# Four PSUM slots for attention scores in tiles 0 to 3, and four score units in a row behind a group's last transposition

## The reference, cut to what matters

```python
s_c = einsum('btghd,bngd->bghtn', qg, kc) * scale + bias       # compressed blocks of 64 keys
s_s = einsum('btghd,bgtkcd->bghtkc', qg, k_s) * scale + bias   # selected blocks (16 of 16 here: all earlier keys)
s_w = einsum('btghd,bkgd->bghtk', qg, kw) * scale + bias       # a window of 512 keys
p = softmax(where(allowed, s, -1e30)); o = p @ v               # for each of the three
y = (g_c * o_c + g_s * o_s + g_w * o_w) * silu(z)
```

## Time and profile before

| what | value |
|---|---|
| median of three executions | 1130.91 us (1128.89 to 1138.05) |
| the profiled execution | 1135.59 us, span 1133.8 us, mean granted TensorE clock 0.958 |
| PE busy | 1067.4 us, 94% of the span |
| DVE, ACT, POOL busy | 585.9, 450.5, 180.7 us |
| prompt attention | from 353.2 us (first score) to about 648 us |

### The profile page before, as it was taken

The page is one execution under the profiler, slowest core; times in us unless marked ns, Lnnn a source line. Parts: engine busy times, 40 slices in busy tenths (PEclk is TensorE's granted clock), DMA queues, the critical chain, the costliest instruction groups (busy, mean ns, idle before and its releaser), DMA issues. The chain is left out here.

```text
span 1133.8 us, 15415 instructions
## 1 busy us (share of the span) xinstructions
PE 1067.4 (94%) x5985; PEld 931.0 (82%) x5985; DVE 585.9 (52%) x1121; ACT 450.5 (40%) x761; POOL 180.7 (16%) x259
## 2 busy tenths in 40 slices
PE   6999999999998889999999888999999999999996
PEld 4889889999997667787777675788799899998884
DVE  4544221123322468787788534544589756555213
ACT  4331121110033457677667504122257655564101
POOL 2110568000004222220200000000112000000000
PEclk9999999999998689999999955999999999999999
DMA  8361002121114000000002620322320111131222
GB/s 295 118 211 63 19 4 63 38 55 39 39 38 149 1 1 1 1 1 1 1 12 64 203 96 1 130 79 94 108 65 19 38 56 39 38 149 61 84 89 79
DMA packets 64566, 74.82 MB, mean 66 GB/s; under 512 B 13793, under 2 KB 48657, under 8 KB 64494
## 3 DMA queue, kind: packets, MB, share of 16 engines
q1 hardware_dynamic: 61902, 70.77, 19.6%
q0 software_dynamic: 2496, 3.04, 0.8%
q10 hardware_dynamic: 96, 0.03, 0.0%
HBM read 62.19 MB, written 16.34 MB: 69 GB/s over the span
## 5 line engine op out<-in xcount | busy, mean ns | idle before, releaser
L1380 PE MATMUL ps<-h1T_hi,w_c_hl 128*128 128x352 f32 x768 | 148.7, 326 | 2.6 <-DVE h1T_lo L2265 1.5
L1380 PE MATMUL ps<-hT_hi,w_fm_hl 128*128 128x352 f32 x768 | 145.5, 324 | 1.5 <-DVE region_w L1988 1.5
L1380 PEld LDWEIGHTS ps<-h1T_hi,w_c_hl 128*128 128x128 f32 x768 | 127.9, 188 | 4.8 <-ACT region_w L1347 1.7
L1384 PE MATMUL ps<-ident,region_w 128*128 128x128 f32 (+2 forms) x730 | 117.7, 290 | 14.6 <-ACT region_w L1194 6.8
L1380 PEld LDWEIGHTS ps<-hT_hi,w_fm_hl 128*128 128x128 f32 x768 | 127.4, 188 | 2.0 <-issue 2.0
L1384 PEld LDWEIGHTS ps<-ident,region_w 128*128 128x128 f32 (+2 forms) x730 | 95.6, 151 | 39.8 <-DVE p_hl L2166 9.3
L2166 DVE TENSOR_TENSOR p_hl<-ps,p_hl 128x512 fp32r<-128x512 f32 x132 | 91.2, 691 | 60.4 <-ACT p_hl L1202 58.9
L1202 ACT CAST p_hl<-ps 128x512 fp32r<-128x512 f32 x132 | 77.1, 584 | 78.8 <-PE ps L1384 78.3
L1380 PE MATMUL ps<-p_hl,v_hl 128*128 128x512 f32 x264 | 96.9, 449 | 7.1 <-DVE p_hl L2166 2.8
L1194 ACT ACTIVATE region_w<-region_w,negm 128x640 f32<-128x640 f32 (+7 forms) x128 | 94.0, 736 | 8.6 <-DVE negm L2141 7.2
L2141 DVE CUSTOM_DVE_ANT_0 region_w<-ps,region_w 128x640 f32<-128x640 f32 (+7 forms) x128 | 88.6, 699 | 5.8 <-PE ps L1380 5.4
(11 more groups left out here) (309 smaller groups left out, 1803.0 us busy)
## 6 DMA issues: line engine op xcount, KB each, us to landing
region_w<-in_x_prompt SPq DMA_DIRECT2D x16, 512.0 KB, 3.7
region_w<-in_w_in_c SPq DMA_DIRECT2D x16, 512.0 KB, 3.8
region_w<-in_w_in_a SPq DMA_DIRECT2D x12, 512.0 KB, 3.8
rel_rows_dram<-rel_line_dram SPq DMA_DIRECT2D x8, 576.0 KB, 12.8
region_y<-in_w_in_a SPq DMA_DIRECT2D x8, 512.0 KB, 6.4
region_w<-rel_rows_dram SPq DMA_DIRECT2D x16, 256.0 KB, 5.1
region_w<-in_w_out_a SPq DMA_DIRECT2D x2, 2048.0 KB, 12.4
x_dram<-region_w SPq DMA_DIRECT2D x8, 512.0 KB, 2.6
```

What stands on the lines that cost most here:

```text
L1380: return nc.tensor.matmul(out, l, r, start=start, stop=stop, skip_group_check=True)
L1384: return nc.tensor.transpose(out, x, ident[0:k, 0:k])
```

## The change

The score units of tiles 0 to 3 (units 0 to 67, none over 512 keys) get four slots of one bank each; unit n waits for the reading of unit n-4. From unit 68 on the two slots of two banks stay; unit 68 waits for unit 64, and unit 69 for unit 67. `FEW` goes from 2 to 4, and with it the order in tiles 2 and 3: all units of group j+2 stand behind the last transposition of group j where group j+1 is of tiles 0 to 3.

```diff
-FEW = 2
+FEW = 4
+NARROW = 17 * (WIN // P)
+
+def score_slot(n):
+    return n % 4 if n < NARROW else 2 * (n % 2)
+
+def slot_free(n):
+    if n < NARROW + 1:
+        return max(0, n - 3)
+    return n - 1
...
-                    slot = 2 * (n % 2)
-                    if n >= 2:
-                        pe.wait_ge(logits_ready, n - 1)
+                    slot = score_slot(n)
+                    if slot_free(n):
+                        pe.wait_ge(logits_ready, slot_free(n))
...
-                    slot = 2 * (n % 2)
+                    slot = score_slot(n)
                     if n == HPG + 2:
                         v_low(1, v_w)
                     dve.wait_ge(scores_done, n + 1)
```

## The result

The changed kernel takes 1152.01 us (median of four runs, 1146.18 to 1153.41) where the kernel before, timed beside it, takes 1130.03: a ratio of 1.0181, 95% interval 1.0142 to 1.0221. It is slower, and above the range of the prediction. The profiled execution took 1150.86 us with a span of 1149.1.

A forecast was written before the change was run, and what follows sets the result against it. PE, busy 94% of the span, was taken as the bound. From the profiled 1135.6 us, -13.2 (slots), +12.2 (bunch) and +1.6 (clock) gave 1136.2, less 4.7 for the median: 1131.5 us, range 1124 to 1139.

The forecast's parts named there:

- Tiles 0 and 1, four slots: Tiles 0 and 1: units start earlier, with fewer waits for readings and less time at the low clock; 13.2 us gained.
- the new wait ahead of the fifth unit: Tile 2's first bunch has five units; the fifth, S38, waits for the reading of S34: 2.1 us.
- Tiles 2 and 3, the bunch: Second cast behind four exponentials lengthens each group's chain: tile 2 +4.5 us, tile 3 +7.7, together +12.2.
- The clock there: Tiles 2 and 3: work behind idle gaps of PE runs at the lower clock; +1.6 us, ends 0 and 13.2.
- The clock falls in tile 3: Rival, chance 0.13: each group's gap brings 1.2 GHz in tile 3, tile 2 loses half as much; 1148.5 us.
- The banks buy nothing: Rival, chance 0.12: cast and exponentials set the pace in tiles 0 and 1, the 13.2 us stay away; 1144.7 us.
- The bunch is hidden: Rival, chance 0.18: the second subtraction's wait is covered by PE work, tiles 2 and 3 keep 59.6 us; 1117.7 us.

The follow-up runs named there:

- the fillers: Kernel before, with 22, 12 and 22 unread transpositions of the identity on PE where it waits ahead of S28, S32 and S36: 1130.18 us against 1134.56, ratio 0.9957.
- the copy first: Changed kernel, with ACT copying the finished group before the four exponentials in groups 8 to 15: 1131.83 us, ratio 0.9963 to the kernel before.

## Why the prediction was wrong, step by step

- **Tiles 0 and 1, four slots: right.** Forecast 13.2 us, measured 15.0 in the changed kernel and 16.7 with the slots alone. T8.0 was forecast near 401 and came at 399.44. Of this T4.0 gave 5.7 (forecast 4.5) and tile 1 gave 9.3 (3.9 + 4.8). Within tile 1 two errors point opposite ways, which is luck: by the fillers the clock is worth 3.65 us, not 4.8, and the new wait ahead of the fifth unit came to 0.6 us (`lc`), not 2.1.
- **Tiles 2 and 3, the bunch: the step that failed.** The sum of +12.2 was made along one chain: the second cast behind four exponentials, its subtraction, the values V(j,1). This chain was sized well. With the copy first, tiles 2 and 3 are +4.5 and +8.2 us longer than before, where +4.5 and +7.7 were forecast. In tile 3 it fits by groups too: 9.30, 9.56 and 22.23 us from T12.0, T13.0 and T14.0 on, where 9.65, 9.1 and 21.9 were forecast. What was left out is a second thing that stands behind the same four exponentials, the copy, and who waits for it. The prediction had the copy's end, 4.46 us behind a group's first transposition, and gave it to "back" in group 12 alone. V(j,0) needs it in every group: V14.0 starts 4.66 us after T14.0 (461.99 to 466.65). On PE T(j,2) stands behind it. The sum put this at nothing; it made eight waits of 20.0 us, and the place of the copy cost 18.8 us. The trace of before had it in view at the end of tile 1, where units stood in fours: ahead of V7.0 PE waits 0.73 us for a copy that ACT makes behind four exponentials (410.82 to 413.21).

```profile
413.93 0.70 PE L1380 MATMUL ps<-p_hl,v_hl 128*128 128x512 f32 x2 [0.73 <-ACT part_sb L1211]
```

- **The clock there: mis-sized, for the same reason.** Forecast +1.6, on the ground that the idle time in half of the groups is spread over short waits. With waits of 2.5 to 3.7 us in six of the eight groups the clock averages 0.80 and 0.82, and costs some 13 us by the estimate above, 7.3 at the least.
- **The whole, between the kernel with four slots alone and the changed one**, tiles 2 and 3 (58.1 to 91.1 us, 33.0): copy behind the exponentials 18.8, some 13 of it through the clock; second cast behind the exponentials 5.6; units in fours on PE and DVE 8.6.
- **Rivals.** *The clock falls in tile 3* (1148.5, chance 0.13) comes nearest in time, and the clock did fall: to 0.82 in tile 3, where its mark was "under about 0.8". It is half right. Of the 17 us that it added to the forecast some 13 were lost to the clock, but behind waits for the copy, which no rival had; the waits for the second subtraction, from which its gaps came, don't show. That its sum comes near is in part luck: it gives tile 2 +9.9 and tile 3 +20.9 us, and +15.9 and +15.6 were measured. *The banks buy nothing* is refuted: the slots alone give 0.9823 and 0.9857. What the Trainium skill, "TensorE: Matmul & The Clock Gate", section "HAM oscillation — how this bites in real kernels", tells of one kernel, that double-buffered PSUM gave no further gain, doesn't carry over to this one, where PE waited 11.3 us for the readers of its slots. *The bunch is hidden* is refuted by the order alone, 1.0355.

## What to carry to other kernels

When work is bunched on an in-order engine, list everything that now stands behind the bunch and who waits for each, not only the one that feeds the known chain: a copy of 0.57 us that empties a bank cost 18.8 us in eight groups. Compare PE's busy time for the same work too: it tells how much of a loss is the clock (here about two thirds) and how much is waiting. Test the halves of a change apart, since here one gained 1.8% and the other lost 3.6%. Where PE must wait and a PSUM bank is free, unread work through the wait can hold the clock: in three kernels here, with waits of 0.4 to 3.7 us, it gave about 0.4% to 1%.

## What the runs showed that was not expected

Two waits alike, 3.15 us (before V12.0) and 3.16 us (before V14.0), had different prices: behind the first the clock stayed at 1.00, behind the second PE worked at 0.50 for some 12 us without a break. It repeats: in the second execution of the changed kernel the clock is 1.00 from 446 to 448 and 0.50 from 466 to 478 again. What decides between the two was not found.
